# The last input projection of a hybrid block runs with its channel blocks outermost, and output weights move up

## What is computed

```python
h = rmsnorm(x, norm_mix)
proj = h @ w_in                        # 1024 -> 2048 columns, four groups of 512
x_lru, g_lru, v_cm, g_cm = split(proj)
c = causal_depthwise_conv(x_lru, conv4_w, conv4_b)          # width 4
r, i = sigmoid(heads(c) @ w_a + b_a), sigmoid(heads(c) @ w_x + b_x)
log_a = -8 * r * softplus(-lam)
a = exp(log_a)
y_lru = scan(a, sqrt(-expm1(2 * log_a)) * (i * c)) * gelu(g_lru)
d = causal_depthwise_conv(v_cm * sigmoid(g_cm), dw31_w, dw31_b)   # width 31
y_cm = silu(layernorm(d, cm_ln_g, cm_ln_b))
x = x + concat(rmsnorm(y_lru), rmsnorm(y_cm)) @ w_out       # 1024 -> 1024
# then: x + (silu(h @ w_gate) * (h @ w_up)) @ w_down, h = rmsnorm(x); a final rmsnorm
```

## Time and profile before

| | |
|---|---|
| median of the runs (2119.1, 2119.61, 2123.15) | 2119.61 us |
| the profiled execution | 2121.55 us |
| its span | 2119.8 us |
| TensorE busy | 2056.3 us, 97% of the span |
| VectorE, ScalarE, GpSimd busy | 927.3, 659.5, 674.2 us |
| last pair of the first stage on TensorE | 402.94 to 426.1 us |
| first matmul of the output projection | 452.7 us |

### The profile page before, as it was taken

One profiled execution on the slowest core, in us unless ns is written; L12 is line 12 of the kernel. 1 busy time (PEld: TensorE's weight loads), 2 busy tenths in 40 slices (PEclk: granted clock), 3 DMA queues, 4 the chain that ended last, 5 costly groups with the idle time before them and its releaser, 6 DMA issues.

```text
span 2119.8 us, 22397 instructions
## 1 busy us (share of the span) xinstructions
PE 2056.3 (97%) x9130; PEld 1698.7 (80%) x9130; DVE 927.3 (44%) x1068; ACT 659.5 (31%) x792; POOL 674.2 (32%) x233
## 2 busy tenths in 40 slices
PE   6999999969999999999999999999999999999997
PEld 5887787847888888888888888888888888888886
DVE  5999899987644221222212222142222122221224
ACT  5466765664533111111121111231111111112112
POOL 2576559764523221212122121212212121211210
PEclk9999999979999999999999999999999999999999
DMA  5223232167853121111212121481211111121101
GB/s 157 58 79 101 80 99 61 59 208 246 250 170 95 44 60 40 44 55 40 59 40 59 40 59 40 139 277 40 59 40 58 41 41 58 40 59 40 40 0 79
DMA packets 189111, 172.42 MB, mean 81 GB/s; under 512 B 5854, under 2 KB 161502, under 8 KB 189066
## 3 DMA queue, kind: packets, MB, share of 16 engines
q1 hardware_dynamic: 189066, 171.81, 26.1%
HBM read 138.24 MB, written 33.55 MB: 81 GB/s over the span
## 4 chain that ended last, share of the span: by engine, by line
PE 90%; DVE 4%; POOL 2%; ACT 1%; issue 1%; DMA 1%; SPq 1%; DVEq 0%; POOLq 0%; ACTq 0%
PE ps L1334 26%; PE ps L1335 26%; PE ps L1336 26%; PE acc L1336 4%; PE acc L1335 4%; PE acc L1334 4%; DVE acc L1223 1%; PE ps L1359 1%; DVE wo_lo L1162 1%; PE ps L1490 1%; POOL w_lo L546 1%; DMA ny<-y_scr 0%; DVE cv L1151 0%; DVE nrs L1132 0%; DVE hn L1310 0%
## 5 line engine op out<-in xcount | busy, mean ns | idle before, releaser
L1334 PE MATMUL ps<-h_hi,wf_hi 128*128 128x512 f32 x1408 | 548.7, 390 | 0.0
L1336 PE MATMUL ps<-h_hi,wf_lo 128*128 128x512 f32 x1408 | 548.5, 390 | 0.0
L1335 PE MATMUL ps<-h_lo,wf_hi 128*128 128x512 f32 x1408 | 548.4, 390 | 0.0
L678 POOL TENSOR_TENSOR wf_lo<-w_raw,wf_hi 128x2048 fp32r<-128x2048 f32 x44 | 202.7, 4606 | 757.8 <-ACT wf_hi L958 757.8
L1280 DVE TENSOR_TENSOR act_gate<-act_gate,ps 128x512 f32<-128x512 f32 x88 | 60.5, 687 | 788.4 <-PE ps L1336 788.4
L1336 PEld LDWEIGHTS ps<-h_hi,wf_lo 128*128 128x128 f32 x1408 | 264.5, 188 | 54.6
L1334 PEld LDWEIGHTS ps<-h_hi,wf_hi 128*128 128x128 f32 x1408 | 264.5, 188 | 54.6
L1335 PEld LDWEIGHTS ps<-h_lo,wf_hi 128*128 128x128 f32 x1408 | 264.5, 188 | 54.6
L1223 DVE SCALAR_TENSOR_TENSOR acc<-glu,par,acc 128x1024 f32<-128x1024 f32 x232 | 299.0, 1289 | 7.2
L1025 ACT CAST f_hi<-act_gate 128x512 fp32r<-128x512 f32 x88 | 54.6, 620 | 495.8 <-DVE act_gate L1280 495.8
L674 POOL TENSOR_TENSOR wd_lo<-wd_raw,wd_hi 128x2048 fp32r<-128x2048 f32 x22 | 101.2, 4602 | 336.1 <-ACT wd_hi L964 336.1
(11 more groups left out here) (170 smaller groups left out, 2745.0 us busy)
## 6 DMA issues: line engine op xcount, KB each, us to landing
w_raw<-in_w_gate SPq DMA_DIRECT2D x44, 512.0 KB, 4.1
w_raw<-in_w_up SPq DMA_DIRECT2D x44, 512.0 KB, 5.2
wd_raw<-in_w_down SPq DMA_DIRECT2D x22, 1024.0 KB, 4.8
w_raw<-in_w_in SPq DMA_DIRECT2D x32, 512.0 KB, 5.3
xt<-in_x SPq DMA_DIRECT2D x16, 512.0 KB, 3.8
x<-in_x SPq DMA_DIRECT2D x16, 512.0 KB, 6.6
out_block<-hn SPq DMA_DIRECT2D x16, 512.0 KB, 2.8
d_scr<-dst SPq DMA_DIRECT2D x8, 512.0 KB, 6.0
```

The costliest lines, as they stand in the source:

```text
L678: g.tensor_tensor(wf_lo[b][:, :, :, :], w_raw[b][:, :, :, :], f32(wf_hi[b][:, :, :, :]), ALU.subtract).then_inc(s_wlo, 1)
L1334: pe.matmul(bank, lhs[0](c), rhs[0](c), start=first, stop=False)
L1335: pe.matmul(bank, lhs[0](c), rhs[1](c), start=False, stop=False)
L1336: mm = pe.matmul(bank, lhs[1](c), rhs[0](c), start=False, stop=last)
```

## The change

The last pair (q = 15) no longer goes through `pair` but through `last_pair`: `k` is the outermost loop, so that the four banks take turns at each channel block and all finish behind the last block. Behind blocks 1, 3 and 5 TensorE counts `s_krow` up: two rows of the input have then been used for the last time. `w_out_hi(0)` to `(2)` wait for that count instead of the pair's end. `w_out_hi(0)` and `(1)` move into the last unit's list, ahead of the `xl` copy, together with `two_minus(6)` and `root(6)`; `w_out_hi(2)` and `(3)` move ahead of `gates(7)`. On VectorE the places of the four lo parts go from 12, 14, 17, 19 to 8, 13, 19, 21 and the scan's from 11 to 12. `gates_tile(6, 1)` stands behind nine matmuls of the last pair, before behind fifteen.

```diff
--- before.py
+++ after.py
@@ -195,6 +195,7 @@
         s_wlo = sem("w_lo_ready")
         s_pair = [sem(f"pair_done{b}") for b in range(4)]
         s_free = [sem(f"pair_free{b}") for b in range(4)]
+        s_krow = sem("h_row_last_used")
         s_tap0 = sem("tap0_done")
         s_prod = sem("short_products_ready")
         s_cadd = sem("short_taps_added")
@@ -264,11 +265,11 @@
 
 
         SCAN_AT, CENTRE_AT, LATE_AT = 22, 16, 27
-        W_OUT_AT = (12, 14, 17, 19)
+        W_OUT_AT = (8, 13, 19, 21)
         CENTRE_AT_LAST, ROW0_AT = 16, 24
         X_NORM_AT = (7, 8, 9, 10, 12, 13, 14, 15)
         X_LO_AT = (9, 10, 11, 12, 14, 15, 16, 17)
-        SCAN_AT_LAST = 11
+        SCAN_AT_LAST = 12
         NORM_STEP = {2: 2, 3: 5}
 
         TURN_FIRST = {(1, 0, 0): 0, (1, 0, 4): 1, (1, 1, 0): 2, (1, 1, 4): 3}
@@ -848,6 +849,19 @@
                     act.wait_ge(s_aux_done[1], aux_g(u - 1, NS - 1) + 1)
                 a.copy(c_hi[:, :], cv[u % 2][:, :]).then_inc(s_chi, 1)
 
+            def w_out_hi(n):
+
+                q = PPAIRS + n
+                act.wait_ge(s_w[q % 2], 32 * (q // 2 + 1))
+                if n < WOQ - 1:
+                    act.wait_ge(s_krow, n + 1)
+                else:
+                    act.wait_ge(s_pair[3], PPAIRS)
+                for e in range(2):
+                    ins = a.activation(wo_hi[:, 2 * n + e], w_raw[q % 2][:, e].rearrange("p k c -> p (k c)"),
+                                       ACT.Copy, scale=w_out_gain(2 * n + e))
+                ins.then_inc(s_whi, 1)
+
             act.wait_ge(s_init, 9)
             for g in range(3):
                 x_std(g)
@@ -877,6 +891,11 @@
                         x_std(g)
                 if u == N0 + 2:
                     norm_swish(0)
+                if u == UNITS - 1:
+                    two_minus(u - 1)
+                    w_out_hi(0)
+                    root(u - 1)
+                    w_out_hi(1)
                 evacuate(u, 0, False)
                 if u == NJ - 1:
 
@@ -887,7 +906,7 @@
                     x_hi(TPH + 2)
                     x_hi(TPH + 3)
                     x_std(TPH + 5)
-                if u >= 1:
+                if 1 <= u < UNITS - 1:
                     two_minus(u - 1)
                 evacuate(u, 1, False)
                 short_product(u, 3)
@@ -914,17 +933,6 @@
                 if u == N0 + 2:
                     norm_rms_cm(0, 6)
 
-            def w_out_hi(n):
-
-                q = PPAIRS + n
-                act.wait_ge(s_w[q % 2], 32 * (q // 2 + 1))
-                if n == 0:
-                    act.wait_ge(s_pair[3], PPAIRS)
-                for e in range(2):
-                    ins = a.activation(wo_hi[:, 2 * n + e], w_raw[q % 2][:, e].rearrange("p k c -> p (k c)"),
-                                       ACT.Copy, scale=w_out_gain(2 * n + e))
-                ins.then_inc(s_whi, 1)
-
             def y_split(w):
                 act.wait_ge(s_yl[w % 2], 32 * (w // 2 + 1))
                 if w >= 2:
@@ -932,15 +940,13 @@
                 a.copy(y_hi[yb(w)][:, :, :], y_raw[yb(w)][:, :, :]).then_inc(s_yhi, 1)
 
 
-            w_out_hi(0)
-            w_out_hi(1)
+            w_out_hi(2)
+            w_out_hi(3)
             gates(UNITS - 1)
             act.wait_ge(s_fin, UNITS - 1)
             y_split(0)
             gate_functions(UNITS - 1)
-            w_out_hi(2)
             two_minus(UNITS - 1)
-            w_out_hi(3)
             squares_lru(1)
             y_split(1)
             squares_cm(1)
@@ -1442,7 +1448,30 @@
                     if r == 2 * NJ - 1 and h + 1 < NH and (st, e, k) in TURN_FIRST:
                         turn_x((h + 1) * TPH + TURN_FIRST[st, e, k])
 
-                pair(w_hi[q % 2], w_lo[q % 2], h_hi, h_lo, q if q else None, tiles if r == 0 else None, turn)
+                if q == PPAIRS - 1:
+                    last_pair(q)
+                else:
+                    pair(w_hi[q % 2], w_lo[q % 2], h_hi, h_lo, q if q else None, tiles if r == 0 else None, turn)
+
+            def last_pair(q):
+
+                whi, wlo = w_hi[q % 2], w_lo[q % 2]
+                for b in range(4):
+                    pe.wait_ge(s_free[b], q)
+                for k in range(KD):
+                    for st in range(NS):
+                        cols = slice(st * TILE, (st + 1) * TILE)
+                        for e in range(2):
+                            if (st, e, k) == (1, 1, 0):
+                                gates_tile(q // 2 - 1, 1)
+                            mm = product(ps[2 * st + e],
+                                         (lambda k: whi[:, e, k], lambda k: wlo[:, e, k]),
+                                         (lambda k: h_hi[:, k, cols], lambda k: h_lo[:, k, cols]),
+                                         [k], start=k == 0, stop=k == KD - 1)
+                            if k == KD - 1:
+                                mm.then_inc(s_pair[2 * st + e], 1)
+                    if k < KD - 1 and k % 2 == 1:
+                        mm.then_inc(s_krow, 1)
 
             def gates_ready(u):
                 pe.wait_ge(s_clo, u + 1)
```

## The result

The kernel after takes **2142.06 us** (median of 4 runs, 2141.4 to 2143.8), the kernel before 2121.26 us (4 runs beside them, 2119.1 to 2123.15). The ratio is 1.01, with a 95% interval of 1.0088 to 1.0112: slower by 20.8 us. The forecast was slower, with +14.3 us and a range up to 2140.0; the time lies 2.1 above that range.

A forecast was written before the change was run, and what follows sets the result against it. The prediction took the input of scan(6), then VectorE's list, as the bound. Its terms 0.4 + 11.6 + 2.3 made +14.3 us on an execution of 2121.55, giving a median of 2133.9 us, range 2127.6 to 2140.0.

The forecast's parts named there:

- Step 1: Input of scan(6): ScalarE's longer list delays the first xl copy, so scan(6) starts 6.6 us later, at 442.1.
- Step 2: VectorE from scan(6) to the centring: less work stands between, so it could centre only 0.4 us later.
- Step 3: Wait for the mean: gates(7) stand behind late-loaded W2 hi and W3 hi; centring 12.0 us later, VectorE idling some 11.6.
- Step 4: Row 0 added inside the convolution: VectorE's fourth add waits for TensorE's second group after W3 lo, +2.3 us.
- The rest of the list is the same: VectorE's remaining list, W2 and W3 lo included, was given no extra cost.
- The sum: Whole kernel: 0.4 + 11.6 + 2.3 = +14.3 us, forecast median 2133.9 us.
- Costed at nothing: Last pair's bank wait, matmul count, extra table load and TensorE's longer idle: together priced at 0, bound 2 for the idle.
- the clock: Rival: four interleaved banks drop TensorE's last pair to 1.2 GHz, 21.8 us longer, total 2152.3 us; chance 0.02.
- Rivals: Other outcomes weighed against the forecast (0.78): hole filled 0.04, first shift only 0.04, nothing 0.02, slow landings 0.10, clock 0.02.
- the filled hole: Rival: work moved into VectorE's idle time before scan(6) saves 4.9 us, total 2114.7 us; chance 0.04.
- the first shift alone: Rival: load 3 in by 445, no wait for the mean, only 0.4 + 2.3 us, total 2122.3 us; chance 0.04.
- Slow landings: Rival: load 3 of the output weights lands 6.1 us later still, total 2140.0 us; chance 0.10.

The follow-up runs named there:

- e2: The kernel before with only the last pair's new matmul order; output weights and VectorE's places left as they were: 2126.63 us, ratio 1.0023.
- e5: The kernel after with root(6) and W1 hi taken back behind unit 7's copies and products, W0 hi left ahead: 2135.73 us, ratio 1.0073.
- e1: The kernel after with gates(7), the split of y row 0 and the gate functions back ahead of W2 hi and W3 hi: 2124.33 us, ratio 1.0016.
- e10: The kernel after with load 3 of the output weights issued only when W2 hi is done: 2146.39 us, ratio 1.0117.
- e11: The kernel after with load 2 issued first and alone, the store of unit 6's y and load 3 behind W2 hi: 2145.94 us, ratio 1.0119.
- e3: The kernel after with GpSimd's fold beside W3 lo cut to 32 of 512 columns, the other sums left out: 2139.45 us, ratio 1.0087.
- e7: The kernel after with loads 2 and 3 right behind the norm input's load, and VectorE's places moved (scan(6) at 18): 2113.14 us, ratio 0.9964.
- e6: The kernel before with VectorE's places alone changed, seven more taps ahead of scan(6): 2115.81 us, ratio 0.9972.
- e9: The kernel after with loads 2 and 3 early, fold before scan input, only the last pair's second half interleaved, ScalarE and VectorE places moved: 2109.64 us, ratio 0.9954.
- e4: The kernel after with load 2 of the output weights issued ahead of the store of unit 6's y: 2141.41 us, ratio 1.0089.

## Why the prediction was wrong, step by step

- **Step 1, scan(6) +6.6:** right. Measured +6.1 (32.6 to 38.7), at 441.87 where 442.1 was said. The matmul order alone makes 4.9 of it (e2), ScalarE's longer list 2.2 over the bank (e5), where I had 3.1, and `two_minus`, no longer among the copies, gives 1.1 back. About half of the 0.5 between forecast and measurement is the table load of the root, which ran while GpSimd's L589 was still at work; I had put it behind.
- **Step 2, centring +0.4 without the wait:** right within 0.8 us, and with the wrong sign. W1 lo took the assumed 3.61, but VectorE was ready for the centring at 51.6 from t0, in the kernel after as in e1, 0.4 ahead of the 52.1 before. That e1's centring then came at +0.5 was luck: it is a wait for the mean. The reading behind the 3.61 was also loose: 2.47 and the rest of the product of 440.01, which is 1.33, make 3.80.
- **Step 3, the wait for the mean:** right in its mechanism (e1), **mis-sized in its landing time**. Load 2 was to be in at 454 and the sigmoid at 459.7; they came at 455.95 and 461.94. I took the 3.7 of the earlier trace rows, from loads issued 7.9 us apart, for loads issued 1.9 us apart with a store just ahead, and added about half a microsecond for the store, which costs 1.2 (e10, e11). From t0 the centring is 14.3 late where 12.0 was said: 2.3 more, of which 2.0 are there at the sigmoid and the rest is a slower mean. VectorE's wait was 14.70 us where 11.6 was said.
- **Step 4, the add's wait +2.3:** right, 1.75.
- **"The rest of the list is the same" (step 4):** this was the step that failed most. W2 and W3 lo together went from 6.08 to 11.29 us, **+5.2**. The prices of a pair in the earlier trace rows were 2.47, 3.61 and 5.50 and step 2 used them for W1, but for W2 and W3 I never asked what GpSimd does at their new time. The wait for the mean set both engines off together: GpSimd's gate products wait for the same late sigmoids. e3 shows by experiment 2.06 of the 5.2 us; the rest is read from the trace. A pair with no GpSimd instruction beside it took 2.48 us each time (W0 in the kernel after, in e1 and in e3 to e5, W0 and W1 in e7). The Trainium skill, "SBUF — State Buffer", section "Who interferes with whom", gives the rule with which this could have been worked out; the trace agrees: 2.47 clear, plus 2.34 for L608, plus the fold, which ran 2.37 in the kernel before, makes 7.2 as a bound, and 6.71 was measured.
- **The sum** by its parts: -0.4 + 14.7 + 1.75 + 5.2 = 21.3 from t0 to scan(7) and to `hn`, and 20.8 in the medians; forecast were 0.4 + 11.6 + 2.3 + 0 = 14.3. The 1.65 us by which the kernel before measured longer this time also count in the 2142.06.
- **Costed at nothing:** held, but for the clock behind the idle time, which made the mean 0.2 us longer (4.02 against 3.83). **Rivals:** the filled hole, the first shift alone and the clock (1.00 from 402 to 426) are false. Slow landings was nearest: its +6.1 priced a worse queue than the 2.0 seen at the sigmoid, and it came near by luck only, since the contention made up the rest. The upper bound of +18 is 2137.6 for the median, inside the range's end of 2140.0; the measured +20.8 lies above both. Its one allowance for GpSimd, 1.9 us, was put on W1, which GpSimd did not hit harder than assumed, and none on W2 and W3, which it did.

## What to carry to other kernels

When a change lets a chain of several engines slip together, price each two-input VectorE instruction behind it again by what GpSimd does at the new time; "the rest is the same" holds only for engines that share nothing. Work that waits for a late transfer must stand behind all work on its engine that the path needs: e1 gave back 18 of 20.8 us by one swap. And look at what stands in front of a wait before moving anything else: taps that wait for nothing, put ahead of the late scan, gave 4.8 us to the kernel before (e6). The best two kernels also load early what uses the freed storage (e7) and get the first bank out early (e9); how much of their gain is owed to each of these was not separated.

## What was not expected of the hardware

- The same 1 MB load took 4.5, 5.7 or 6.8 us from issue to use: alone, with a 0.5 MB store just ahead, and with a second 1 MB load issued 1.9 us behind it as well. So a later issue on the queue slows an earlier one.
- One pair of 128x1024 `scalar_tensor_tensor` took between 2.47 and 6.77 us (e10) by GpSimd's work beside it. GpSimd pays as well: its 128x1024 instructions, 2.35 clear, took 3.3 to 3.4 there. Four in a row, with a GpSimd instruction beside the first and one beside the last, took 6.01 (e7), 1.5 each.
- The eight matmuls of the mean took 3.67 us (e5), 3.83 (before), 4.02 (after), 4.56 (e1) and 5.29 (e4), at granted clocks of 0.98, 0.94, 0.89, 0.79 and 0.68 over them, each time behind idle time on TensorE and six gate matmuls at 0.50, the 1.2 GHz level. In all but the kernel before the centring waits for them, so a burst that is the same on paper moved it by up to 1.6 us.
